# Two-layer hybrid decoder step: the passage from the projections to the attention, reordered

## The chip, the cores and the metric

The kernel runs on one core of one Trainium2 chip. The metric is the device time of one execution in microseconds (us), the median of the runs made; three runs of the kernel before gave 1884.6 us (1883.93 to 1886.74). Engines: PE (TensorE; PEld is its weight load), DVE (VectorE), ACT (ScalarE), POOL (GpSimd) and SP (SyncE), which issues all DMAs.

## The reference

One inference step over 2048 prompt tokens and 64 decode tokens (8 sequences of 8), width 1024, all float32.

```python
# layer 0
a, gl, z = split(rms_norm(x) @ w_in_a, 3)
v = a * sigmoid(gl)                       # causal depthwise convolution, width 31, over positions
c = silu(layer_norm(conv(v))) * silu(z)
x1 = x + c @ w_out_a
# shared keys and values, once
k, v = split(rms_norm(x1, g_kv) @ w_kv, 2)     # 4 heads of 64 each; k = rms_norm(k) per head
# layer 1
q, z = split(rms_norm(x1, g_b) @ w_in_b, 2)    # 16 heads of 64; q = rms_norm(q) per head
s = q @ k.T / 8 - slope * distance             # window of 128 positions, learned sink per head
o = softmax_with_sink(s) @ v
y = x1 + (o * silu(z)) @ w_out_b
```

Outputs are y of prompt and decode tokens, the convolution's last inputs, and the last 128 keys and values of the prompt (`k_p`, `v_p`) and of each decode sequence (`k_s`, `v_s`).

## The kernel before

**Stages.** `phase_a` computes layer 0's input projections and most of the convolution. `phase_b` goes over 17 token tiles (16 of 128 prompt tokens, and tile 16, the 64 decode tokens): for each, LayerNorm, gates, output projection (`out`), residual, RMSNorm, and the projections of k/v and q (`qkv`). Its outputs go to scratch tensors in DRAM: `x1_d`, `kv_d`, `q_d`, and `ht_d`, the normalised and transposed activations in two parts. `phase_c` goes over the 16 prompt tiles: it loads q, k, v and `ht_d` of the tile, transposes q and k on PE, computes the layer-1 gate z, attention, and the layer-1 output projection of the tile before; the decode sequences are fitted in between. Each engine runs its own instruction list; the lists are joined by semaphores, and the order on each engine is the order in which the functions below are called.

**Projections** (`project`, L119). Each float32 operand is cut into a high and a low part, and a 512-column projection is 24 matmuls of three products over 8 slices of the contraction. Weights are cut once: SP loads 256 KB pieces into a staging buffer (`split_weights_dma`, L84), ACT writes the high part (`split_weights_hi`, L99), DVE the low part (`split_weights_lo`, L107). With s stages, a piece's load waits until DVE is through with the piece s before it. A 1024x512 weight matrix is 8 pieces.

**Weight slots.** Five slots of 32 KB per partition. In `phase_b` they hold OUT0, OUT1, KVS, Q0, Q1, in this order; slot 4 is its own tile `b_w`. In `phase_c` slots 0 and 1 hold the gate weights Z0 and Z1, slots 2 and 3 the output weights OUT0 and OUT1, and the memory of slot 4 holds attention's working tiles: the transposed q (`c_qt`) and k (`c_kt`), the scores (`c_s`), the gate (`c_sz`) and others. The staging buffer of the gate weights has 3 stages and lies in `b_cz`; the one of the output weights has 4 and lies over `b_ht`.

**Passage, before.** The last steps of `phase_b` treat tile 15's q and k (`queries`, `keys`, `query_sums`) and tile 16. PE: `out(16)`, `qkv(15)`, `turn_h(16)` (L1248), `qkv(16)`, then `turn_q(0)` (L1868) and `turn_k(0, 0)` (L1874), then the first attention tile: `qk(0)` (L1937), `z(0, 0)`, `qk(1)`, `turn_p(0)` (L1946), `z(0, 1)`, `pv(0)` (L1955, L1961), `qk(2)`, `turn_p(1)`, `pv(1)`, the decode tokens' turns (L1881) and gate projections (`decode_z`), and so on. ACT copies the transposed q and k out of PSUM (L1541, L1545) after its last step of `phase_b`, `queries(16)`, which waits for `qkv(16)`. SP: all 16 gate pieces, with the loads of tile 0 (`first_loads`) before the last 5; the store of `ht_d` of tile 16; then a wait for that store and for the last matmul of `qkv(16)`, 4 output-weight pieces, the stores of tile 16 (among them 16 small ones to `k_s` and `v_s`), 7 loads for the decode tokens, the loads of tile 1, and the further output-weight pieces. ACT and DVE cut the output weights two pieces at a time (`split(0)`, `split(2)`, ... in the bodies of `phase_c`) between the steps of the first attention tile; `split(0)` stands ahead of the first scores on DVE (L1687) and the first exponentials on ACT (L1559, L1561), `split(4)` ahead of the second exponentials.

## Time and profile before

| | |
|---|---|
| median of 3 runs | 1884.6 us |
| the profiled execution's own time | 1884.13 us |
| its span in the trace | 1882.3 us |
| PE busy | 1748.9 us (93%) |
| mean granted TensorE clock | 0.97 of full |
| `phase_b`, tiles | from 0.69 ms to 1.22 ms of the span |
| `phase_c` | from 1.22 ms to the end |

Times in the rows below are microseconds from the span's start. PEclk is the granted TensorE clock, 1.00 for 2.4 GHz and 0.50 for 1.2 GHz; a stretch between holds both.

### The profile page before, as it was taken

The numbers are of one execution on the slowest core, as the hardware profiler recorded it, in microseconds if no ns is written. First come the engines' busy times: TensorE is split into PE (matmuls) and PEld (weight loads), VectorE is DVE, ScalarE is ACT, GpSimd is POOL, SyncE is SP. The second block draws the span as 40 slices with busy tenths as digits, with TensorE's granted clock in tenths as the row PEclk, the third lists the DMA queues.
The fourth block names the chain that finished last, engine by engine and source line by source line (L and its number), as shares of the span: only waits on it lengthen the run. The fifth ranks groups of instructions, "written<-read, shape, count | busy, mean of one in ns | idle before, by whom it ended". The sixth has DMA issues, their size and how long they took to land.

```text
span 1882.3 us, 25336 instructions
## 1 busy us (share of the span) xinstructions
PE 1748.9 (93%) x9105; PEld 1421.9 (76%) x9105; DVE 1199.6 (64%) x2013; ACT 848.6 (45%) x1658; POOL 590.9 (31%) x446
## 2 busy tenths in 40 slices
PE   7999999999997377999999999779999999999998
PEld 6798988888886356787888887557777777777776
DVE  6378889898997445785666643345555556655553
ACT  5555655555563352232323232345444554445442
POOL 2399999999993002221121211100000000000000
PEclk9999999999999588999999999979999999999999
DMA  6221211111212545334444432552221232222311
GB/s 200 81 73 39 73 37 51 57 44 61 64 39 100 167 137 202 137 109 123 137 134 131 148 124 100 175 162 87 82 87 64 76 107 72 93 71 82 101 49 40
DMA packets 157228, 184.47 MB, mean 98 GB/s; under 512 B 55189, under 2 KB 120829, under 8 KB 152972
## 3 DMA queue, kind: packets, MB, share of 16 engines
q1 hardware_dynamic: 157116, 183.00, 30.0%
q8 instruction: 67, 1.10, 0.2%
q14 instruction: 45, 0.37, 0.1%
HBM read 115.31 MB, written 70.34 MB: 99 GB/s over the span
## 4 chain that ended last, share of the span: by engine, by line
PE 54%; DMA 5%; DVE 3%; ACT 2%; SPq 1%; issue 1%; POOL 1%; DVEq 0%; ACTq 0%; POOLq 0%
PE c_acc L119 19%; PE b_pso L119 12%; PE b_psq L119 9%; PE c_pss L1937 3%; PE c_psp L1946 3%; PE c_pso L1961 3%; DMA ht_d<-b_ht 1%; PE b_pst L1248 1%; DVE b_x L1114 1%; PE c_pso L1955 1%; PE b_psc L1242 1%; PE c_pst L1868 1%; DMA b_cz<-in_w_in_b 1%; PE c_pss L119 1%; DMA b_three<-v_left 1%
## 5 line engine op out<-in xcount | busy, mean ns | idle before, releaser
L687 PE MATMUL a_ps<-a_xt,a_wring 128*128 128x512 f32 (+3 forms) x2880 | 556.4, 354 | 13.6 <-ACT a_zo L509 9.3
L687 PEld LDWEIGHTS a_ps<-a_xt,a_wring 128*128 128x128 f32 x2880 | 494.3, 189 | 70.3 <-ACT a_zo L509 11.4
L446 POOL TENSOR_TENSOR a_csum<-a_prod,a_csum 128x704 f32<-128x704 f32 (+1 forms) x242 | 425.5, 1758 | 42.9 <-ACT a_prod L496 7.5
L588 DVE SCALAR_TENSOR_TENSOR a_pst<-a_vbuf,taps,a_pst 128x704 f32<-128x704 f32 (+1 forms) x352 | 327.6, 931 | 11.0
L496 ACT ACTIVATE a_prod<-a_vbuf,taps 128x704 f32<-128x704 f32 (+1 forms) x264 | 225.7, 865 | 182.5 <-POOL a_csum L446 168.5
L119 PE MATMUL b_pso<-w,b_yt 128*128 128x512 f32 (+1 forms) x816 | 193.1, 396 | 0.3 <-DVE b_yt L1108 0.3
L119 PE MATMUL c_acc<-w,c_ht 128*128 128x512 f32 x768 | 185.9, 398 | 0.2 <-issue 0.2
L119 PEld LDWEIGHTS b_pso<-w,b_yt 128*128 128x128 f32 (+1 forms) x816 | 151.7, 188 | 35.3 <-DVE b_yt L1108 0.7
L119 PE MATMUL c_acc<-w,c_ot 128*128 128x512 f32 x720 | 172.0, 394 | 0.0
L119 PEld LDWEIGHTS c_acc<-w,c_ht 128*128 128x128 f32 x768 | 143.3, 190 | 36.5 <-issue 7.3
L119 PEld LDWEIGHTS c_acc<-w,c_ot 128*128 128x128 f32 x720 | 132.9, 188 | 32.5 <-issue 5.8
L1567 ACT ACTIVATE c_pt<-c_psp 128x1024 f32<-128x1024 f32 (+1 forms) x64 | 63.9, 998 | 141.0 <-PE c_psp L1946 141.0
L1561 ACT ACTIVATE c_s<-c_s,c_nm 128x256 f32<-128x256 f32 (+1 forms) x256 | 124.5, 488 | 0.1
L119 PE MATMUL b_pso<-w,b_ht 128*128 128x512 f32 (+1 forms) x408 | 102.6, 409 | 10.3 <-DVE b_x L1114 7.9
L119 PE MATMUL b_psq<-b_w,b_ht 128*128 128x512 f32 (+1 forms) x408 | 99.1, 398 | 5.5 <-DVE b_w L107 5.4
L119 PEld LDWEIGHTS b_pso<-w,b_ht 128*128 128x128 f32 (+1 forms) x408 | 77.6, 194 | 31.6 <-issue 12.5
L1687 DVE SCALAR_TENSOR_TENSOR c_s<-c_dist,c_pss 128x256 f32<-128x256 f32 (+1 forms) x256 | 88.1, 406 | 15.1 <-PE c_pss L1937 14.0
L948 POOL TENSOR_TENSOR b_hms<-b_hss,rms_eps 128x4 f32<-128x4 f32 (+3 forms) x34 | 9.7, 285 | 274.5 <-DVE b_hss L1142 159.6
L119 PE MATMUL b_psq<-w,b_ht 128*128 128x512 f32 (+1 forms) x408 | 95.3, 389 | 0.0
L119 PEld LDWEIGHTS b_psq<-b_w,b_ht 128*128 128x128 f32 (+1 forms) x408 | 76.1, 188 | 25.4 <-DVE b_w L107 8.2
L1006 ACT ACTIVATE b_qo<-b_x 128x1024 f32<-128x1024 f32 (+1 forms) x17 | 18.0, 1061 | 167.6 <-DVE b_x L1114 167.6
L119 PEld LDWEIGHTS b_psq<-w,b_ht 128*128 128x128 f32 (+1 forms) x408 | 75.3, 185 | 17.3
(182 smaller groups left out, 2158.7 us busy)
## 6 DMA issues: line engine op xcount, KB each, us to landing
ht_d<-b_ht SPq DMA_DIRECT2D x16, 1024.0 KB, 4.7
c_ht<-ht_d SPq DMA_DIRECT2D x16, 1024.0 KB, 4.8
a_stage<-in_w_in_a SPq DMA_DIRECT2D x24, 512.0 KB, 4.0
a_x<-in_x_prompt SPq DMA_DIRECT2D x16, 512.0 KB, 3.4
b_cz<-c_d SPq DMA_DIRECT2D x16, 512.0 KB, 4.9
b_cz<-z_d SPq DMA_DIRECT2D x16, 512.0 KB, 6.7
b_x<-in_x_prompt SPq DMA_DIRECT2D x16, 512.0 KB, 3.5
x_d<-b_x SPq DMA_DIRECT2D x16, 512.0 KB, 2.6
```

What stands on the lines that cost most here:

```text
L119: last = pe.matmul(out, xt[:, a, k, 0:n], w[:, b, k], start=(k == 0 and a == 0 and b == 0), stop=(k == KT - 1 and b == 1))
L446: pool.tensor_tensor(out, prod[:, (PTAPS * n + i) % RING, 0:t1 - t0], out, ALU.add).then_inc(prod_added, 1)
L496: act.activation(prod[:, m % RING, 0:t1 - t0], vbuf[:, b % 2, t0 + k:t1 + k], ACT.Identity, scale=wcol(k, b), bias=bcol(b) if i == 0 else ...
L588: dve.scalar_tensor_tensor(part if k == DTAPS - 1 else here, vbuf[:, b % 2, t0 + k:t1 + k], wcol(k, b), part if k == 0 else here, ALU.mult ...
L687: last = pe.matmul(out, wring[:, u % 3, a, k], xt[c][:, e, k, 0:n], start=(k == 0 and a == 0 and e == 0), stop=(k == KT - 1 and a == 1))
L1114: dve.tensor_tensor(x[0:n], ps_o[0:n], x[0:n], ALU.add).then_inc(x1_ready, 1)
L1561: ins = act.activation(s[:, b, j, ks], s[:, b, j, ks], ACT.Exp, bias=nm[:, b, j:j + 1], accum_out=den[:, b, j:j + 1])
L1567: act.activation(pt[:, ks], ps_p[:, ks], ACT.Copy).then_inc(pt_ready, 1)
L1687: ins = dve.scalar_tensor_tensor(s[:, b, place(j), ks], dist[:, gap], -slope[kv * GROUP + j], ps_s[:, place(j), ks], ALU.mult, ALU.add)
L1937: ins = pe.matmul(ps_s[:, place(j), keys_of(t)], qt[e * HD:(e + 1) * HD, h // 2], keys[:, keys_of(t)], start=True, stop=True)
L1946: ins = pe.transpose(ps_p[:, half, j], s[:, b, j, half * P:(half + 1) * P], g.ident[:, :])
L1961: ins = pe.matmul(ps_o[e * HD:(e + 1) * HD, 0:2 * P], v[:, half, kv * HD:(kv + 1) * HD], pt[:, half, 2 * e:2 * e + 2], start=(half == 0), ...
```

## The change

Six things are altered, all around the end of `phase_b` and the first attention tile:

1. **Slots.** KVS goes to slot 4 and Q1 to slot 2. So attention's tiles lie over the k/v weights, which are last read by the first 24 matmuls of `qkv(16)`.
2. **Turns inside.** `turn_q(0)` and `turn_k(0, 0)` are issued on PE inside `qkv(16)`, between its k/v and its q projections; ACT's copies of them follow its `keys_values(16)`.
3. **Order.** Tile 15's q steps come later on ACT and DVE, behind `cut_h(16)`; the body of tile 16 ends before them. ACT and DVE cut the gate weights in the order 5, 3, 2, 6 pieces between these steps.
4. **Gate weights.** A staging buffer of 4 stages, over two stages of `b_three` and half of `b_cz`; pieces are counted on `phase_c`'s semaphores (0 to 15), output weights after them (16 to 31).
5. **SP's queue.** Tile 0's q is loaded once x1 of tile 16 is stored, its k after `turn_h(16)`, the rest of its loads after gate piece 11. `kv_d` of tile 16 is stored before the wait for the last q matmul; SP waits for that store to land and then writes `k_s` and `v_s` with 2 DMAs from `kv_d` to DRAM in place of 16. The output-weight pieces go 6 (of which 2 wait for stages), then the store of q and the decode loads, then 2 more ahead of tile 1's loads, then the rest.
6. `qscale` is computed at the start of `phase_b`; small tiles (sinks and others) get other places.

The core of the diff:

```diff
@@ phase_b
-    OUT0, OUT1, KVS, Q0, Q1 = range(5)
+    OUT0, OUT1, Q1, Q0, KVS = range(5)
-    gate_stage = cz[:, 0:w.stages * HALF].rearrange("p (s n) -> p s n", s=w.stages)
+    gate_stage = nc.alloc_sbuf_tensor_at("b_gate", [P, 4, HALF], F32, offset=g.w_base + 4 * g.slot_bytes + p.at["three"] + 4 * HALF)
@@ phase_b, sync: body(t)
+            if isinstance(t, int) and t == TILES:
+                for done in (ht_out, q_out, kv_out):
+                    sp.wait_ge(done, 16 * (TILES - 1))
...
             if isinstance(t, int) and t == TILES:
-                sp.wait_ge(tc_done, ALL)
-                sp.wait_ge(prod_ready, ALL)
-                w.stage = gate_stage
-                split_weights_dma(sp, io.w_in_b[:, D:D + HALF], w, 3)
-            if not (isinstance(t, int) and t == 0):
-                store_qkv(t - 1)
+                return
+            store_kvq(t - 1)
@@ phase_b, sync: the end
-        split_weights_dma(sp, io.w_in_b[:, D + HALF:2 * D], w, 4, k1=w.stages)
-        sp.wait_ge(ht_out, 16 * TILES)
-        sp.wait_ge(q_out, 16 * TILES)
-        sp.wait_ge(kv_out, 16 * TILES)
+        sp.wait_ge(tc_done, ALL)
+        sp.wait_ge(prod_ready, ALL)
+        gates(0, 4)
         sp.wait_ge(x1_out, 16 * ALL)
+        sp.wait_ge(h_ready, ALL)
+        load_queries()
+        store_kvq(TILES - 1)
+        sp.dma_start(io.k_p, kvo[:, 0:KV]).then_inc(copy_out, 16)
+        sp.dma_start(io.v_p, kvo[:, KV:2 * KV]).then_inc(copy_out, 16)
+        gates(4, 8)
         sp.wait_ge(th_done, ALL)
-        first_loads()
-        split_weights_dma(sp, io.w_in_b[:, D + HALF:2 * D], w, 4, k0=w.stages)
+        load_keys()
         store_ht(ALL - 1)
-        p.store_last = lambda: store_qkv(ALL - 1)
+        gates(8, 12)
+        load_rest()
+        store_q(TILES - 1)
+        gates(12, 16)
+        store_kvq(ALL - 1)
+        sp.wait_ge(kv_out, 16 * ALL)
+        for to, cols in ((io.k_s, slice(0, KV)), (io.v_s, slice(KV, 2 * KV))):
+            sp.dma_start(to[:, P - DS:P, :], g.kv_d[SEQ:TOK, cols].rearrange("(b i) n -> b i n", b=DB)).then_inc(copy_out, 16)
+        p.store_last = lambda: store_q(ALL - 1)
@@ phase_b, scalar: the end
         steady(act, body)
+        act.wait_ge(out_mm, ALL)
+        gates(0, 5)
         cut_h(ALL - 1)
-        split_weights_hi(act, 0, gains[Q0], w, 3, k0=5)
-        split_weights_hi(act, 1, gains[Q0], w, 4, k1=w.stages)
+        queries(TILES - 1)
+        gates(5, 10)
         keys_values(ALL - 1)
-        split_weights_hi(act, 1, gains[Q0], w, 4, k0=w.stages)
+        turned()
+        gates(10, 16)
         queries(ALL - 1)
@@ phase_b, vector: the end
         steady(dve, body)
+        gates(0, 5)
         cut_h(ALL - 1)
-        queries(ALL - 2)
-        split_weights_lo(dve, 0, gains[Q0], w, 3, k0=5)
-        split_weights_lo(dve, 1, gains[Q0], w, 4, k1=w.stages)
+        query_sums(TILES - 1)
+        gates(5, 8)
+        queries(TILES - 1)
+        gates(8, 10)
         keys(ALL - 1)
-        split_weights_lo(dve, 1, gains[Q0], w, 4, k0=w.stages)
+        gates(10, 16)
         query_sums(ALL - 1)
@@ phase_b, tensor
             project(pe, ps_o[0:n, 0:HALF], ht, w.wslot[KVS], n, (w.w_lo, 0) if gate else None).then_inc(kv_mm, 1)
+            if between is not None:
+                between()
             after(pe, q_ready, t)
@@ phase_c, sync
-        split_weights_dma(sp, io.w_out_b[:, 0:HALF], w, 0, k1=w.stages)
+        w.stage = stg
+        split_weights_dma(sp, io.w_out_b[:, 0:HALF], w, 2, k1=6)
         prev.store_last()
         sp.wait_ge(prev.q_out, 16 * ALL)
-        sp.wait_ge(prev.kv_out, 16 * ALL)
-        sp.wait_ge(prev.w.w_lo, 5 * KT)
+        sp.wait_ge(w.w_lo, 2 * KT)
...
+            if first:
+                split_weights_dma(sp, io.w_out_b[:, 0:HALF], w, 2, k0=6)
             if not last:
                 load_q(t + 1)
                 load_k(t + 1, 1 - r)
             if first:
-                split_weights_dma(sp, io.w_out_b[:, 0:HALF], w, 0, k0=w.stages)
                 load_v(1, 1)
+                split_weights_dma(sp, io.w_out_b[:, HALF:D], w, 3, k1=4)
                 load_ht(1)
-                split_weights_dma(sp, io.w_out_b[:, HALF:D], w, 1)
+                split_weights_dma(sp, io.w_out_b[:, HALF:D], w, 3, k0=4)
@@ phase_c, scalar and tensor
+        def turned():
+            act.wait_ge(prev.qscale_made, 1)
+            queries(0)
+            keys(0, 0)
+        def first_turns():
+            turn_q(0)
+            turn_k(0, 0)
-        prev.tensor(pe)
-        turn_q(0)
-        turn_k(0, 0)
+        prev.tensor(pe, first_turns)
```

`gates(first, stop)` loads, or cuts the high or low parts of, the gate-weight pieces from `first` up to `stop`; `store_kvq(t)` stores `kv_d` and, for tiles before 15, `q_d`; `load_rest` loads the distance tables, the sinks, `ht_d` and v of tile 0.

## Rows read from the trace of the kernel before

**Rows 1.** The page: PE's busy time, the chain that ended last by engine.
```profile
PE 1748.9 (93%) x9105; PEld 1421.9 (76%) x9105; DVE 1199.6 (64%) x2013; ACT 848.6 (45%) x1658; POOL 590.9 (31%) x446
...
PE 54%; DMA 5%; DVE 3%; ACT 2%; SPq 1%; issue 1%; POOL 1%; DVEq 0%; ACTq 0%; POOLq 0%
```
**Rows 2.** Windows of 1300 to 1882 us: busy us per engine, PEclk, DMA share, GB/s.
```profile
1300.00:1882.00 582.00, 571.70 (x3273) 427.56 (x3271) 318.04 (x812) 267.69 (x757) 0.00 (x0) 1.00 0.23 77
```
**Rows 3.** Timeline, PE, end of phase_b: start, duration, operation, count, idle before.
```profile
1177.33 5.70 PE L119 MATMUL b_pso<-w,b_ht 128*128 128x512 f32 x24 [1.40 <-DVE b_x L1114]
1182.87 5.60 PE L119 MATMUL b_psq<-w,b_ht 128*128 128x512 f32 x24
...
1196.88 7.30 PE L119 MATMUL b_pso<-w,b_ht 128*64 128x512 f32 x24 [2.32 <-DVE b_ht L1119]
1204.02 5.68 PE L119 MATMUL b_psq<-w,b_ht 128*64 128x512 f32 x24
```
**Rows 4.** Timeline, DVE, between the transposes of tile 16 and its projections.
```profile
1195.00 1.22 DVE L1142 TENSOR_REDUCE b_hss<-b_qo 128x16 f32<-128x1024 f32 x1 [2.43 <-ACT b_qo L1038]
1196.14 0.68 DVE L1119 TENSOR_TENSOR b_ht<-b_pst,b_ht 128x512 fp32r<-128x512 f32 x1
1199.54 1.23 DVE L1148 TENSOR_TENSOR b_qo<-b_psq,b_hrs 128x1024 f32<-128x1024 f32 x1 [2.72 <-POOL b_hrs L950]
```
**Rows 5.** Timeline, PE, the passage and the first attention tile up to `z(0, 1)`.
```profile
1215.05 1.04 PE L1868 MATMUL c_pst<-ident,c_q 128*128 128x128 f32 x8
1215.93 0.60 PE L1874 MATMUL c_acc<-ident,c_kd 128*128 128x128 f32 x4
1225.23 1.23 PE L1937 MATMUL c_pss<-c_kt,c_qt 64*128 64x128 f32 x8 [8.70 <-ACT c_kt L1545]
1226.38 8.03 PE L119 MATMUL c_acc<-w,c_ht 128*128 128x512 f32 x24
1234.35 0.72 PE L1937 MATMUL c_pss<-c_kt,c_qt 64*128 64x128 f32 x8
1234.99 0.66 PE L1946 MATMUL c_psp<-ident,c_s 128*128 128x128 f32 x4
1235.87 5.72 PE L119 MATMUL c_acc<-w,c_ht 128*128 128x512 f32 x24 [0.22 <-issue]
```
**Rows 6.** Windows, the first gate projection, `z(0, 0)`; columns as in rows 2.
```profile
1226.40:1234.40 8.00, 8.00 (x28) 6.10 (x26) 3.62 (x10) 3.61 (x11) 0.26 (x1) 0.70 0.35 98
```
**Rows 7.** Timeline, SP's DMA issues: time of issue, time issuing, what.
```profile
1217.07 0.62 SPq L829 DMA_DIRECT2D ht_d<-b_ht  x1
1222.32 1.75 SPq L84 DMA_DIRECT2D c_stg<-in_w_out_b  x4
...
1231.18 0.47 SPq L856 DMA_DIRECT2D q_d<-b_qo  x1
...
1241.25 1.93 SPq L84 DMA_DIRECT2D c_stg<-in_w_out_b  x4
```
**Rows 8.** Timeline, ACT, in the first attention tile.
```profile
1226.35 0.63 ACT L99 ACTIVATE w<-c_stg 128x512 fp32r<-128x512 f32 x1 [0.75 <-DMA c_stg<-in_w_out_b]
1229.69 1.28 ACT L1559 ACT_TABLE_LOAD   x1 [2.71 <-DVE c_es L1698]
...
1234.45 0.60 ACT L1553 ACTIVATE c_sz<-c_acc 128x512 f32<-128x512 f32 x1 [1.72 <-PE c_acc L119]
...
1246.03 1.38 ACT L99 ACTIVATE w<-c_stg 128x512 fp32r<-128x512 f32 x2 [9.46 <-DMA c_stg<-in_w_out_b]
```
**Rows 9.** Timeline, PE, after the second stop of the first attention tile.
```profile
1249.10 1.12 PE L1946 MATMUL c_psp<-ident,c_s 128*128 128x128 f32 x4 [6.05 <-ACT c_s L1561]
...
1255.09 7.33 PE L119 MATMUL c_acc<-w,c_otd 128*64 128x512 f32 x24
...
1263.82 5.74 PE L119 MATMUL c_acc<-w,c_otd 128*64 128x512 f32 x24 [0.15 <-DVE c_early L1732]
```
**Rows 10.** DMA issues, 1140 to 1300 us: tile 16's store to `kv_d`, KB, us to landing.
```profile
kv_d<-b_three SPq DMA_DIRECT2D x1, 128.0 KB, 5.0
```

More of the change, by code:

```diff
@@ L1268, in out, with qkv @@
             ins.then_inc(out_mm, 1)
-        def qkv(t, gate=False):
+        def qkv(t, gate=False, between=None):
             n = rows_of(t)
@@ L1339, in phase_c @@
     nsink = sb("c_nsink", [P, HEADS])
+    small[0] = prev.at["three"] + 4 * HALF
     sinkd = sb("c_sinkd", [P, 2])
```

100 lines of the change are left out of this document (52 added, 48 removed).

## The prediction

> **What bounds the kernel now.** The page comes first: PE is busy 93% of the span and carries 54% of the chain that ended last, all others together a quarter of that [rows 1]. So time is gained only where PE stands still or runs slowly. The windows come next: from 1300 us on PE is busy 571.7 of 582 us at the full clock [rows 2]. Nothing there is touched by the change, so what is gained ahead of it is carried to the end unchanged. Last comes PE's timeline through the passage. The reader is to see four things. Tile 16's k/v projection waits 2.32 us and then starts to start takes 7.14 us (1196.88 to 1204.02), where tile 15's takes 5.54 (1177.33 to 1182.87) [rows 3]. After the turns of q and k PE stands for 8.70 us, on ACT's copy of k [rows 5]. The gate projection behind it takes 7.97 us, at a mean clock of 0.70: part of it ran at 1.2 GHz [rows 6]. And PE stops again for 6.05 us before the second `turn_p`, with a projection of 7.33 us following [rows 9]. These are about 17 us of standing and 6 us of slow clock.
>
> The sum is made against the profiled execution (1884.13 us). It lies 0.5 below the median of 1884.6, and I add that back at the end.
>
> **Part 1: tile 16's cut goes ahead of tile 15's q.** In the kernel before, DVE reduces tile 15's squares at 1195.00 (1.22 us) and only then makes the low part of tile 16 at 1196.14; PE follows 0.74 us later [rows 4]. PE had finished the transposes at 1194.56 (1196.88 less 2.32). After the change the chain is ACT's high part (a 512-column copy, 0.60 [rows 8]) plus the handover, DVE's cut at 1195.2, PE at 1195.95. Removed: 0.93 us. The clock: PE resumed at full speed after 1.40 us of standing, at half speed after 2.32 [rows 3]. The new stop is 1.39 us, nearest to the first, so I take 5.54 us instead of 7.14: 1.60 more (bounds 0 and 1.60). PE starts the k/v part at 1195.95 and ends it at 1201.49.
>
> What is moved here must still be in time. Five gate pieces stand ahead of `cut_h(16)` on ACT. The fifth has to wait for a stage; it is loaded once DVE has cut the first (about 1187) and SP has stored tile 15's k and v (until 1187.6), so it lands near 1191.5 and is cut by 1192.3, 2 us ahead of the transposes. Tile 15's query chain (squares, reduction, POOL, product) took 4.54 us from reduction to product [rows 4]. Now the reduction is at 1196.1, so the product is at 1200.65 and ends at 1201.9; PE wants `q_ready` at 1202.9. Slack 1.0 us, and the three gate pieces that DVE takes meanwhile (1197.3 to 1199.3) fit in. On SP, `ht_d` of tile 15 now waits for a landing, some 2.5 us, which nobody misses before 1194.
>
> **Part 2: turns inside the last projection, copies over the k/v slot.** The turns cost PE the same 1.48 us (1215.05 to 1216.53 [rows 5]), now in front of the q part: 1.38 start to start. q was asked for at about 1180.5 and k at 1194.6, and PE turns them at 1201.5 and 1202.4; a load of such a kind lands in about 5 us, so neither is waited for. The q part takes 11.03 us as before (1204.02 [rows 3] to 1215.05 [rows 5]). Its end: 1195.95 + 5.54 + 1.38 + 11.03 = 1213.9. ACT's copies are done at about 1205, under this projection. So the 8.70 us go wholly: the first scores start at 1213.9 instead of 1225.23, and at the full clock take 0.64 (1234.35 to 1234.99) instead of 1.15 [rows 5]. The gate projection starts at 1214.5 and ends at 1220.1, in 5.54 us instead of 7.97. Up to here 14.3 us are gained (1234.35 less 1220.1). The cover: the eight pieces of Z0 are cut by about 1199, those of Z1 by 1214.
>
> **Part 3: what is late next.** Scores need their distance step and exponentials, and ahead of them on DVE and ACT stands `split(0)`: two output-weight pieces. Their staging lies over tile 16's activations, so SP can't ask for them before the last q matmul, 1213.9. In the kernel before SP asked at 1222.32, after the landing of the `ht_d` store issued at 1217.07 [rows 7]; now that store goes at 1196. SP has a new wait, on the landing of `kv_d` of tile 16. Issued at about 1207.9 it lands 5.0 us later by its own row [rows 10], 1212.9; the two DRAM copies behind it aren't in the rows, and I take one issue of 0.44 each (1.75/4 [rows 7]), bounds 0.3 and 1.0. SP is ready at 1213.8. So the piece chain moves by 8.3 us and no more, while PE has moved by 14.3: the exponentials, which ended 3.04 us after the table load began (1229.69 [rows 8], so 1232.73), end at 1224.45. PE, done with `qk(1)` at 1220.95, stands until 1224.55. This is a **new wait of 3.6 us**. Then `turn_p(0)`, ACT's tanh, DVE's product and `z(0, 1)`: 1.42 us from tanh to projection (1234.45 [rows 8], 1235.87 [rows 5]), hence 1225.8. The clock falls, since 3.6 us is longer than the stop of 2.32. After 8.70 us it cost about 3.0 us (0.51 + 2.43); after 2.32 it cost 1.6. I take 2.0 on `z(0, 1)` (bounds 0 and 3.0), ending at 1233.4.
>
> The Trainium skill (DMA: Bandwidth & Descriptors, Anatomy of one DMA) gives a DMA 2.0 us of fixed cost plus its bytes at 436 GB/s, fitted on another issue path. By my estimate from it a 256 KB piece lands in 2.6 us, where the row of ACT's wait has 3.7 (second piece, issued at about 1222.7, cut at 1226.35 [rows 7, 8]). By the page the new wait would be 2.6 us instead of 3.6, and the total 1 us lower; the row is used.
>
> **Part 4: the second stop.** It was `split(4)`: ACT's pieces 4 and 5 came at 1246.03, asked for at 1241.25 behind everything SP did from 1224 on [rows 7, 8]. Six pieces are now asked for ahead of that work; the last two wait only for DVE's first two cuts (about 1219.5). So the 6.05 us and the slow clock behind them go. What is late next is `split(6)` on ACT: pieces 6 and 7 stand behind the q store, its landing and seven decode loads. With the three loads of tile 1's q and k these took from 1231.18 to 1241.25 [rows 7]; now the q store goes at 1222.5, so the two are asked for at 1230.9 to 1231.8 and land at about 1235 to 1236. ACT cuts them, then copies the second transposed scores: PE waits about 1.0 us (bounds 0 and 3). From 1233.4: `pv(0)` 0.9, `qk(2)` 0.65, `turn_p(1)` and the gate's transposes 0.95, the wait 1.0, `pv(1)` 0.65, the decode turns 0.85: the first `decode_z` at 1238.45 instead of 1255.09. It takes 5.55 instead of 7.33, and the next starts at 1245.7 after its usual 1.5 us handover, instead of 1263.82 [rows 9]. **18.1 us.** Later output pieces come with 3 us or more in hand.
>
> **The sum.** 0.93 + 1.60 (part 1), + 8.70 + 0.51 + 2.43 (part 2), + 0.1 of rounding at the turns: 14.3. New wait and slow clock in part 3: -6.2 (1241.4, where `z(0, 1)` ended, less 1233.4 leaves 8.0). Part 4: 6.05 of standing, 2.0 of waiting for the gate product, 1.8 on the projection, 1.3 on small matmuls, less 1.0: +10.1. In all 18.1, hence 1884.1 - 18.1 = 1866.0, and with 0.5 for the median 1866.5 us. Against an error of 0.2% (3.8 us), about what a measurement of this kernel can tell from no change, this is far off zero.
>
> **Rivals.** (a) *SP comes late to the output pieces.* The wait for `kv_d`, or the DRAM copies behind it, last 3 to 5 us longer, or pieces 6 and 7 land later behind the many small decode packets. Each microsecond beyond 1213.9 lengthens the new stop by one. For it: SP's slack is 0.1 us by my reckoning. Against: the store has little beside it. Time 1870.5. The skill speaks for it (same page, same section): the write receipt makes the completion of a DMA that writes HBM surprisingly long. The row's 5.0 us already holds that, beside other traffic.
> (b) *The clock stays at 2.4 GHz* at the new stop, because the pieces land sooner and the stop falls towards 2 us. For it: a stop of 1.40 did no harm. Time 1863.5.
> (c) *The slow clock holds on* (the other side). After the new stop come further short stops (the gate handover, 1.0, 0.5 us), and PE remains at 1.2 GHz up to the end of tile 1's gate projections. In rows 6, 4.8 us at half clock and 3.2 at full did 24 matmuls and some; that is near 11 us for a projection at half clock, 5.4 too many. Five projections add 27 us, less the 2.0 counted, and the small matmuls about 5: 30 us, 1896. It turns slower than before from about three and a half projections on. Against: at 1226.4 the clock came back within one projection.
> (d) *Nothing arrives*: tile 1 would have to wait for its own loads, which stand behind more pieces than before. They need an 18 us delay; q and k are asked for at 1232 and used at 1255. Time 1884.
>
> **Chances.** Forecast 0.70 (1863.5 to 1869), (a) 0.13, (b) 0.11, (c) 0.03, (d) 0.03. The range 1862.5 to 1871.0 takes in (a) and (b) and the bounds above: upwards 1.6 for the clock in part 1, 1.0 in part 3 and 2 in part 4, not all at once. Faster 0.95, same 0.02, slower 0.03.
>
> **What would show it.** Right: tile 16's k/v projection after a stop of about 1.4 us in 5.5 to 5.7 us; no stop after the turns, which stand between k/v and q; `z(0, 0)` in 5.6 us; a stop of about 3.6 us before the first `turn_p`, released by ACT's exponentials; no stop over 2 us after it; from 1245 on the old pattern, 18 us sooner. Wrong: a wait on `q_ready` inside `qkv(16)` (part 1), q or k landing late (part 2), ACT waiting for a piece more than 2 us at `split(6)` (part 4), a clock at half speed through `decode_z` (c).

## The result: 18.2 us faster

| | before | changed |
|---|---|---|
| median | 1885.67 us (4 runs, 1883.93 to 1887.31) | 1867.46 us (4 runs, 1865.19 to 1870.01) |
| the profiled execution's own time | 1884.13 us | 1867.84 us |
| its span | 1882.3 us | 1866.0 us |

The ratio is 0.9904 with a 95% interval of 0.9887 to 0.9921. Forecast were 1866.5 us for the median and 18.1 us of gain. The two profiled executions differ by 16.3 us. The one of before was itself 1.5 below its median, the other 0.4 above.

The page of the changed kernel, PE's busy time and the chain that ended last (rows 1 of before). PE is busy 5.4 us less with the same matmuls, since fewer of them run at the slow clock. The chain's shares barely moved, though nearly 1% of the time has gone.

```profile
PE 1743.5 (93%) x9105; PEld 1421.5 (76%) x9105; DVE 1198.8 (64%) x2013; ACT 847.9 (45%) x1658; POOL 591.2 (32%) x446
...
PE 54%; DMA 4%; DVE 3%; ACT 3%; issue 1%; SPq 1%; POOL 0%; DVEq 0%; ACTq 0%; POOLq 0%
```

A window of the changed kernel over the attention (start:end, length, busy us and instructions per engine, PEclk, DMA share, GB/s). It answers rows 2: PE is busy 570.4 of 581 us at the full clock, as before. What was gained ahead of it was carried to the end.

```profile
1285.00:1866.00 581.00, 570.42 (x3266) 426.56 (x3262) 317.52 (x812) 267.65 (x757) 0.00 (x0) 1.00 0.23 77
```

PE's timeline of the changed kernel through the passage (start, duration, operation, count, idle before and its releaser). It answers rows 3, 5 and 9.

```profile
1164.78 11.29 PE L119 MATMUL b_pso<-w,b_yt 128*64 128x512 f32 x48
...
1196.13 5.73 PE L119 MATMUL b_pso<-b_w,b_ht 128*64 128x512 f32 x24 [1.41 <-DVE b_ht L1132]
1201.70 1.04 PE L1903 MATMUL c_pst<-ident,c_q 128*128 128x128 f32 x8
1202.57 0.60 PE L1909 MATMUL c_acc<-ident,c_kd 128*128 128x128 f32 x4
1202.93 11.29 PE L119 MATMUL b_psq<-w,b_ht 128*64 128x512 f32 x48
1214.14 0.72 PE L1972 MATMUL c_pss<-c_kt,c_qt 64*128 64x128 f32 x8
1214.79 5.75 PE L119 MATMUL c_acc<-w,c_ht 128*128 128x512 f32 x24
1221.87 0.72 PE L1972 MATMUL c_pss<-c_kt,c_qt 64*128 64x128 f32 x8 [1.33 <-DVE c_s L1717]
1226.10 1.08 PE L1981 MATMUL c_psp<-ident,c_s 128*128 128x128 f32 x4 [3.51 <-ACT c_s L1583]
1227.25 7.92 PE L119 MATMUL c_acc<-w,c_ht 128*128 128x512 f32 x24
...
1238.25 0.65 PE L1996 MATMUL c_pso<-c_pt,c_v 128*64 128x256 f32 x4 [0.82 <-ACT c_pt L1589]
...
1239.59 5.75 PE L119 MATMUL c_acc<-w,c_otd 128*64 128x512 f32 x24
...
1247.28 5.74 PE L119 MATMUL c_acc<-w,c_otd 128*64 128x512 f32 x24 [0.70 <-DVE c_early L1762]
...
1259.94 5.74 PE L119 MATMUL c_acc<-w,c_ht 128*128 128x512 f32 x24
```

The reader is to see this. The stop ahead of tile 16's k/v projection (1196.13) is 1.41 us instead of 2.32, and the projection runs at full speed. The turns (1201.70, 1202.57) stand between k/v and q without a stop. The first scores follow the q part at once (1214.14), where 8.70 us were lost. Then come two stops that were not there, 1.33 and 3.51 us, with a slow `z(0, 1)` behind them (7.92 us). The 6.05 us of rows 9 are gone, and 0.82 us is what is left ahead of the second `pv`.

For comparisons between kernels one measure is used below, **the passage**: from the start of tile 16's output projection (b_yt, 128*64) to the start of tile 1's first gate projection. In the changed kernel it is 1259.94 - 1164.78 = 95.16 us. In the kernel before it ran between these two rows of PE's timeline, 111.85 us. So it is 16.7 us shorter by the rows. Where two kernels are compared inside the passage, times are counted from its start, which differs by up to 6.6 us between the traces. It leaves out what happens ahead of it in an execution.

```profile
1164.64 11.29 PE L119 MATMUL b_pso<-w,b_yt 128*64 128x512 f32 x48
...
1276.49 5.73 PE L119 MATMUL c_acc<-w,c_ht 128*128 128x512 f32 x24
```

SP's DMA issues in the changed kernel (time of issue, time issuing, what), answering rows 7:

```profile
1204.19 4.95 SPq L84 DMA_DIRECT2D b_gate<-in_w_in_b  x4
1209.24 0.48 SPq L849 DMA_DIRECT2D kv_d<-b_three  x1
1213.42 0.78 SPq L953 DMA_DIRECT2D out_k_s<-kv_d  x1
1214.24 0.73 SPq L953 DMA_DIRECT2D out_v_s<-kv_d  x1
1215.09 6.20 SPq L84 DMA_DIRECT2D c_stg<-in_w_out_b  x6
```

and ACT in the first attention tile, answering rows 8:

```profile
1217.65 0.63 ACT L99 ACTIVATE w<-c_stg 128x512 fp32r<-128x512 f32 x1 [2.38 <-DMA c_stg<-in_w_out_b]
1219.58 0.63 ACT L99 ACTIVATE w<-c_stg 128x512 fp32r<-128x512 f32 x1 [1.29 <-DMA c_stg<-in_w_out_b]
1222.91 1.28 ACT L1581 ACT_TABLE_LOAD   x1 [2.71 <-DVE c_es L1728]
...
1227.85 1.14 ACT L99 ACTIVATE w<-c_stg 128x512 fp32r<-128x512 f32 x2
```

SP comes to the output-weight pieces at 1215.09. The second of them is cut on ACT at 1219.58, after a wait for its landing. Only then can DVE do the scores' distance step, and ACT loads its table at 1222.91. `turn_p` starts at 1226.10. That is the new wait. The fifth and sixth piece (1227.85) are cut without any.

### The profile page after: what moved, and what is told of

It reads as the page before. It is cut to its first block, busy times and chain, and to the rows that moved or that the text cites. A ratio compares the mean times of both kernels' runs of the same rounds, so it can differ in the third digit from the quotient of the medians.

```text
span 1866.0 us, 25323 instructions
## 1 busy us (share of the span) xinstructions
PE 1743.5 (93%) x9105; PEld 1421.5 (76%) x9105; DVE 1198.8 (64%) x2013; ACT 847.9 (45%) x1658; POOL 591.2 (32%) x446
## 4 chain that ended last, share of the span: by engine, by line
PE 54%; DMA 4%; DVE 3%; ACT 3%; issue 1%; SPq 1%; POOL 0%; DVEq 0%; ACTq 0%; POOLq 0%
PE c_acc L119 19%; PE b_pso L119 12%; PE b_psq L119 9%; PE c_pss L1972 3%; PE c_psp L1981 3%; PE c_pso L1996 3%; PE b_pst L1262 1%; DMA ht_d<-b_ht 1%; DVE b_x L1127 1%; PE c_pso L1990 1%; PE b_psc L1256 1%; PE c_pst L1903 1%; PE c_pss L119 1%; DMA b_three<-v_left 1%; DMA c_stg<-in_w_out_b 1%
## 5 line engine op out<-in xcount | busy, mean ns | idle before, releaser
L119 PE MATMUL b_psq<-w,b_ht 128*128 128x512 f32 (+1 forms) x816 | 189.9, 391 | 4.7 <-DVE w L107 4.7
L119 PEld LDWEIGHTS b_psq<-w,b_ht 128*128 128x128 f32 (+1 forms) x816 | 150.6, 185 | 40.6 <-DVE w L107 6.5
L119 PE MATMUL b_pso<-b_w,b_ht 128*128 128x512 f32 (+1 forms) x408 | 102.3, 408 | 9.3 <-DVE b_x L1127 7.9
L119 PEld LDWEIGHTS b_pso<-b_w,b_ht 128*128 128x128 f32 (+1 forms) x408 | 78.0, 195 | 29.8 <-issue 10.6
L960 POOL TENSOR_TENSOR b_hms<-b_hss,rms_eps 128x4 f32<-128x4 f32 (+3 forms) x34 | 10.1, 297 | 265.3 <-DVE b_hss L1155 158.3
L1750 DVE TENSOR_TENSOR c_sz<-c_pso,c_sz 128x256 f32<-128x256 f32 x64 | 27.1, 424 | 93.7 <-ACT c_sz L1594 93.7
L1178 DVE SCALAR_TENSOR_TENSOR b_conv<-b_conv,taps 128x64 f32<-128x64 f32 x240 | 68.2, 284 | 19.6 <-DVE b_conv L1178 1.1
```

Of the source, the lines that this page charges most:

```text
L119: last = pe.matmul(out, xt[:, a, k, 0:n], w[:, b, k], start=(k == 0 and a == 0 and b == 0), stop=(k == KT - 1 and b == 1))
L1178: dve.scalar_tensor_tensor(out, win, scalar(g.taps, k * KT), out, ALU.mult, ALU.add).then_inc(left_step, 1)
```

## The experiments

**One part undone: tile 15's squares ahead of tile 16's cut** (`cut_behind_q`).

```diff
@@ phase_b, scalar
-        cut_h(ALL - 1)
         queries(TILES - 1)
+        cut_h(ALL - 1)
@@ phase_b, vector
-        cut_h(ALL - 1)
         query_sums(TILES - 1)
+        cut_h(ALL - 1)
```

> The changed kernel with one part undone: on ACT and DVE tile 15's squares and their sums stand ahead of tile 16's cut again. Theory A (the first exponentials hang on output-weight pieces that SP asks for once the last q matmul is done and its own queue is free, at 1215.1 us, 0.95 us after the last q matmul at 1214.14): tile 16's k/v projection starts 0.9 us later after a stop of 2.3 us and takes 7.1 instead of 5.6 us, since the clock falls; the q part ends 2.5 us later, of which SP's 0.95 us swallow a part, so tile 1's first gate projection comes 1.6 us later than in the changed kernel (1259.94). Theory B (PE's own work sets the end throughout): 2.5 us later. If the clock doesn't fall: A 0.0, B 0.9.

PE's timeline of this kernel, tile 16's k/v projection:

```profile
1198.10 7.33 PE L119 MATMUL b_pso<-b_w,b_ht 128*64 128x512 f32 x24 [2.32 <-DVE b_ht L1132]
```

Its stop and its 7.33 us are those of rows 3. The passage is 96.62 us, 1.46 more than in the changed kernel, where theory A gave 1.6 and B 2.5. Median 1868.38 us, ratio to before 0.9917 (0.9900 to 0.9933). Part 1 removes 2.5 us of PE's time and is worth 1.5 by this trace. The rest is swallowed on SP: here it asks for the output pieces 0.14 us after the last q matmul (1217.85 and 1217.71), in the changed kernel 0.95 us after it, so its request moves by only 1.7 us. In the timing the difference of 0.0013 between the ratios (about 2.5 us) lies within the intervals.

**The turns behind the whole last projection again** (`turns_after`).

```diff
@@ phase_b, scalar
-        turned()
         gates(10, 16)
+        turned()
@@ phase_c, tensor
-        prev.tensor(pe, first_turns)
+        prev.tensor(pe, None)
+        first_turns()
```

> The changed kernel with the turns of tile 0's q and k put behind the whole last projection again, and ACT's copies behind its last gate piece; the slots stay as changed. PE's first scores start about 1.9 us later than 1214.14, at 1216.0, after a stop of 1.8 us. Theory A (pieces set the first exponentials, 4.8 us of standing behind them on PE): the stops before the first turn_p shrink by 1.9 us, and tile 1's first gate projection starts within 0.3 us of the changed kernel's 1259.94. Theory B (PE's own work sets the end): 1.9 us later.

PE's timeline: the q part, the first scores, the first `turn_p`, `z(0, 1)`, the second `pv` and the first `decode_z`.

```profile
1202.93 11.26 PE L119 MATMUL b_psq<-w,b_ht 128*64 128x512 f32 x48 [1.05 <-DVE b_qo L1161]
...
1216.90 0.71 PE L1972 MATMUL c_pss<-c_kt,c_qt 64*128 64x128 f32 x8 [1.41 <-ACT c_kt L1567]
...
1226.03 0.63 PE L1981 MATMUL c_psp<-ident,c_s 128*128 128x128 f32 x4 [2.11 <-ACT c_s L1583]
1227.19 5.73 PE L119 MATMUL c_acc<-w,c_ht 128*128 128x512 f32 x24 [0.53 <-issue]
...
1237.80 0.65 PE L1996 MATMUL c_pso<-c_pt,c_v 128*64 128x256 f32 x4 [2.62 <-ACT c_pt L1589]
...
1239.37 7.04 PE L119 MATMUL c_acc<-w,c_otd 128*64 128x512 f32 x24
```

The first scores come at 1216.90, 2.8 us later than in the changed kernel, where 1.9 were expected. Yet `turn_p` comes at 1226.03, in the same place to 0.1 us (both traces have the output projection at 1164.8). The stop ahead of it has shrunk from 3.51 to 2.11, the one before `qk(1)` is gone. `z(0, 1)` then runs at full speed, and the clock falls for the first `decode_z` instead. The passage is 95.68 us, 0.52 more. That is over the 0.3 that theory A allowed and far under the 1.9 of B, and no more than two traces of the changed kernel differ by. The trace shows why PE's lateness is lost again: ACT stood 1.13 and 0.72 us for pieces 6 and 7 ahead of the copy that the second `pv` waits for, and the first `decode_z` starts 74.58 us after the output projection, in the changed kernel 74.81. So theory A's mechanism holds: the part of the change that its name puts foremost is worth next to nothing in this trace, since something else sets the first exponentials and the second `pv`. The timing can't confirm so small a cost: median 1868.66, ratio 0.9918 (0.9902 to 0.9935), 0.0014 or 2.6 us above the changed kernel's with intervals that overlap. The row at 1202.93 shows one thing more. PE waits 1.05 us for `q_ready` ahead of the q part; in the changed kernel the turns fill just that wait.

**SP's order of output pieces as before the change** (`four_pieces_first`).

```diff
@@ phase_c, sync
-        split_weights_dma(sp, io.w_out_b[:, 0:HALF], w, 2, k1=6)
+        split_weights_dma(sp, io.w_out_b[:, 0:HALF], w, 2, k1=4)
...
-            if first:
-                split_weights_dma(sp, io.w_out_b[:, 0:HALF], w, 2, k0=6)
             if not last:
                 load_q(t + 1)
                 load_k(t + 1, 1 - r)
             if first:
+                split_weights_dma(sp, io.w_out_b[:, 0:HALF], w, 2, k0=4)
                 load_v(1, 1)
-                split_weights_dma(sp, io.w_out_b[:, HALF:D], w, 3, k1=4)
                 load_ht(1)
-                split_weights_dma(sp, io.w_out_b[:, HALF:D], w, 3, k0=4)
+                split_weights_dma(sp, io.w_out_b[:, HALF:D], w, 3)
```

> The changed kernel with SP's order of output pieces as before the change: four pieces, the q store, the decode loads, q and k of tile 1, and only then the fifth piece. Theory A (ACT's fifth and sixth piece stand ahead of the second exponentials, and their request is what made the second stop): pieces asked for at about 1234, cut at about 1239, second exponentials done at 1241.6, PE stands some 5 us before the second turn_p and runs slowly after it; tile 1's first gate projection 6 to 8 us later than 1259.94, whole time 1873.5 to 1875.5. Theory B (that stop was a follow-up of the first one and is gone with it): under 2 us later.

PE's timeline, the second `turn_p` and the first `decode_z`; then SP's request for the fifth piece:

```profile
1241.22 1.11 PE L1979 MATMUL c_psp<-ident,c_s 128*128 128x128 f32 x4 [6.49 <-ACT c_s L1581]
...
1247.22 7.26 PE L119 MATMUL c_acc<-w,c_otd 128*64 128x512 f32 x24
```

```profile
1232.15 1.93 SPq L84 DMA_DIRECT2D c_stg<-in_w_out_b  x4
```

The second stop is back with 6.49 us, released by the exponentials, and the slow clock after it, 7.26 us for a projection. Passage 105.48 us, 10.3 more than the changed kernel, where 6 to 8 were expected; median 1876.35, ratio 0.9961 (0.9947 to 0.9976). ACT cuts the fifth piece after 12.17 us of standing, ended by that piece's landing. The mechanism is that of part 4, and the size is what part 4 had put on it (10.1), not the smaller figure of this expectation: the stop was 6.49 us instead of some 5, and another stop of 1.98 us for the gate product follows, which it doesn't name.

**The same order put into the kernel before, alone** (`before_six_pieces`): the diff above, reversed, on the kernel before.

> The kernel before with SP's order of output pieces alone changed (6 pieces ahead of the stores and decode loads, 2 behind them, then q and k of tile 1). Theory A (ACT's fifth piece made the second stop; pieces 6 and 7, asked for at about 1242 behind 16 small stores and the decode loads, are late next): no stop before the second turn_p, one of about 4 us before the second pv; 106 to 108 us on the measure of split0_late, where the kernel before has 111.85; total 1879 to 1881. Theory B (this part is worth by itself what its absence cost in four_pieces_first, 10.3 us): 101.5 us, total 1874.5.

PE's timeline, the second `pv`:

```profile
1248.76 1.12 PE L1963 MATMUL c_pso<-c_pt,c_v 128*64 128x256 f32 x4 [4.77 <-ACT c_pt L1569]
```

Passage 108.21 us, 3.6 less than before; median 1879.37, ratio 0.9975 (0.9965 to 0.9985). That is 0.2 us outside theory A's 106 to 108 and far from B's 101.5. So this part costs 10.3 us where it is missing from the change, but gives only 3.6 where it is added alone: in the kernel before, pieces 6 and 7 stand behind the 16 small stores as well, ACT waits 2.90 and 1.08 us for them, and a stop of 4.77 us takes the place of the one of 6.05. The parts don't add up, and here the timing agrees: by the ratios the same two steps are 0.0057 (10.7 us) and 0.0025 (4.7 us), each clear of its interval.

**The three stages** (`three_stages`): a gate piece is asked for only when the piece three before it is cut.

```diff
@@ phase_c, sync, gates
             for k in range(first, stop):
+                after(sp, w.w_lo, k - 2)
                 split_weights_dma(sp, ...)
```

> The changed kernel with gate piece k asked for only when piece k-3 is cut, as with three stages. Theory A (the gate weights have slack everywhere but ahead of tile 16's cut): SP holds q's load and the k/v store back by about 1 us, the fifth piece lands 1 to 1.5 us later, still ahead of the transposes' end; 95.2 to 95.7 us on the measure of split0_late. Theory B (four stages carry the result): the fifth piece comes later than the transposes, tile 16's cut waits, and the clock falls: 97 us or more.

SP's issues: the last four gate pieces, the k/v store, the output pieces. Then PE: tile 16's k/v projection, `qk(1)`, `turn_p(0)` and `z(0, 1)`.

```profile
1209.77 10.86 SPq L84 DMA_DIRECT2D b_gate<-in_w_in_b  x4
1220.72 0.48 SPq L849 DMA_DIRECT2D kv_d<-b_three  x1
...
1225.55 6.20 SPq L84 DMA_DIRECT2D c_stg<-in_w_out_b  x6
```

```profile
1197.47 7.26 PE L119 MATMUL b_pso<-b_w,b_ht 128*64 128x512 f32 x24 [2.68 <-DVE b_ht L1132]
...
1232.32 1.23 PE L1973 MATMUL c_pss<-c_kt,c_qt 64*128 64x128 f32 x8 [8.93 <-DVE c_s L1718]
1236.55 1.08 PE L1982 MATMUL c_psp<-ident,c_s 128*128 128x128 f32 x4 [3.00 <-ACT c_s L1584]
1237.71 7.62 PE L119 MATMUL c_acc<-w,c_ht 128*128 128x512 f32 x24
```

Theory A was wrong, and B, which had said only 97 us or more, was right for the smaller part: passage 105.68 us, 10.5 more; median 1877.58, ratio 0.9967 (0.9956 to 0.9978). What B said did happen, a cut that comes late (2.68 us of standing, then 7.26 us at a slow clock), but it makes the first scores only 2.8 us later. The larger part is in SP's queue. The last four gate pieces take SP from 1209.77 to 1220.63, where the changed kernel needs 1204.19 to 1209.14, since each request waits for the cut of the piece three before it, not four, and behind them stand the k/v store and the output pieces. These are asked for at 1225.55 instead of 1215.09, 10.5 us later, and the first scores' step with them: PE stands 8.93 us ahead of `qk(1)`. The gate weights themselves were never late: `z(0, 0)` ran without a stop.

**The output pieces ahead of the k/v store's wait and the copies** (`pieces_before_copies`).

```diff
@@ phase_b, sync, the end
         store_kvq(ALL - 1)
-        sp.wait_ge(kv_out, 16 * ALL)
-        for to, cols in ((io.k_s, ...), (io.v_s, ...)):
-            sp.dma_start(to[:, P - DS:P, :], g.kv_d[SEQ:TOK, cols]...)
-        p.store_last = lambda: store_q(ALL - 1)
+        def store_last():
+            sp.wait_ge(kv_out, 16 * ALL)
+            for to, cols in ((io.k_s, ...), (io.v_s, ...)):
+                sp.dma_start(to[:, P - DS:P, :], g.kv_d[SEQ:TOK, cols]...)
+            store_q(ALL - 1)
+        p.store_last = store_last
```

> The changed kernel with the wait for tile 16's k/v store and the two DRAM copies moved behind the six output pieces. Theory A (SP's lateness of 0.95 us at these pieces is passed on in full to the first exponentials): pieces asked for at 1214.35 instead of 1215.09, first turn_p at 1225.35 instead of 1226.10, tile 1's first gate projection 0.7 us earlier. Theory B (the landing, not the request, decides, because other traffic is in the way): no difference, or later, since the copies now run beside the fifth piece.

ACT's cut of the second piece. This trace runs 1.10 us later up to here (the output projection starts at 1165.88).

```profile
1219.04 0.63 ACT L99 ACTIVATE w<-c_stg 128x512 fp32r<-128x512 f32 x1 [0.52 <-DMA c_stg<-in_w_out_b]
```

Passage 93.60 us, 1.56 less: theory A in direction, with twice its 0.7. SP asks at 1215.38, in the changed kernel's time 1214.28, 0.81 earlier. The second piece is cut at 1217.94 in that time instead of 1219.58, 1.64 earlier. So half of what the cut gains is the request, the other half a shorter time from request to landing: 3.66 us instead of 4.49. That the copies made the difference is borne out by the next run, which has no copies and 3.68 us, and by the other five traces with the two copies directly ahead, which have 4.01 to 4.49. Median 1865.67, ratio 0.9901 (0.9883 to 0.9919); against the changed kernel's 0.9904 that isn't a difference that the timing alone could show.

**The copies replaced by 16 small stores** (`sixteen_stores`), with the wait for the k/v store ahead of the q store.

```diff
@@ phase_b, sync, the end
-        sp.wait_ge(kv_out, 16 * ALL)
-        for to, cols in ((io.k_s, ...), (io.v_s, ...)):
-            sp.dma_start(to[:, P - DS:P, :], g.kv_d[SEQ:TOK, cols]...)
+        for b in range(DB):
+            sp.dma_start(io.k_s[b, P - DS:P, :], kvo[rows, 0:KV])
+            sp.dma_start(io.v_s[b, P - DS:P, :], kvo[rows, KV:2 * KV])
```

> The changed kernel with k_s and v_s written by 16 small stores in the place of the two DRAM copies, and the wait for the k/v store moved ahead of the q store. Theory A (the two copies brought nothing in their place: the store at 1209.24 plus 16 issues of 0.34 us ends at 1215.2, the wait and the copies end at 1215.05): 95.2 us within 0.5 on the measure of split0_late. Theory B (the copies' own traffic or the small stores' traffic delays the two pieces that are waited for): 0.8 us or more to either side.

The output pieces in SP's issues (the output projection starts at 1168.09 here):

```profile
1219.61 5.40 SPq L84 DMA_DIRECT2D c_stg<-in_w_out_b  x6
```

They are asked for 51.5 us after the output projection's start, in the changed kernel 50.3. The passage is 95.69 us, 0.53 more; median 1870.28, ratio 0.9927 (0.9907 to 0.9948). In the place where they stand, the wait and two copies save 1.2 us of SP's time over the 16 stores. But the second piece is cut 3.68 us after the request instead of 4.49, so the cut itself comes only 0.4 us later (55.20 and 54.80 us after the start). Theory A's "brought nothing" is right for the end, though not for SP's queue; a difference of 0.53 us in the passage is no more than two traces of one kernel show.

**The changed kernel a second time** (`changed_again`), on the same chip as `sixteen_stores` and `reordered_turns_after`.

> The changed kernel itself, beside the two below. On the measure of split0_late it took 95.16 us in its profile; the first stops hang on landings, so 94.5 to 96.5 us is expected here. The two profiled executions of before and after differ by 16.3 us, the medians by 18.2: if that is scatter of single executions alone, this one again gives a ratio between 0.9887 and 0.9921.

PE's timeline, tile 16's k/v projection:

```profile
1195.76 7.30 PE L119 MATMUL b_pso<-b_w,b_ht 128*64 128x512 f32 x24 [1.41 <-DVE b_ht L1132]
```

Median 1867.17, ratio 0.9909 (0.9890 to 0.9927), passage 95.71 us. The stop is 1.41 us as in the first trace, but this time the clock fell after it, and the projection took 7.30 us instead of 5.73. All the same the passage is only 0.55 us longer, within the 94.5 to 96.5 expected. SP asked for the output pieces 0.84 us later (1215.56; the second copy took 1.42 us of issuing here), the stops ahead of the first `turn_p` shrank from 4.84 to 3.92 us, and `z(0, 1)` lost 0.6 us less to its slow clock (7.32 us instead of 7.92).

**The first two pieces cut behind the first exponentials** (`split0_late`).

```diff
@@ phase_c, scalar
-            split(0)
             exps(t * KVH, 0, ks)
             gate_tanh(t, 0)
+            split(0)
             split(2)
@@ phase_c, vector
-            split(0)
             scores(G, t, 0, 0, r)
...
             gate(t, 0)
+            split(0)
             scores(G + 1, t, 1, 1, r)
```

> The changed kernel with the first two output-weight pieces cut behind the first exponentials and the first gate product on ACT and DVE, SP's order unchanged. Measured from the start of tile 16's output projection to the start of tile 1's first gate projection, the kernel before takes 111.85 us, the changed one 95.16. Theory A (removing the new stop only uncovers the next transfer: pieces 6 and 7 are asked for behind the q store and the decode loads at about 1233, and ACT has them ahead of the second pv): the stop before the first turn_p falls from 4.84 to about 1 us, z(0,1) starts 4 us earlier and at full clock, and PE then stands 5 to 7 us before the second pv; 95 to 97 us, so no gain. Theory B (the new stop was the last one that counts): 88 to 90 us.

PE's first `turn_p`, `z(0, 1)` and second `pv`, then ACT's seventh piece:

```profile
1226.84 0.63 PE L1981 MATMUL c_psp<-ident,c_s 128*128 128x128 f32 x4 [0.77 <-ACT c_s L1583]
1227.99 5.72 PE L119 MATMUL c_acc<-w,c_ht 128*128 128x512 f32 x24 [0.53 <-issue]
...
1244.44 1.12 PE L1996 MATMUL c_pso<-c_pt,c_v 128*64 128x256 f32 x4 [5.74 <-ACT c_pt L1589]
```

```profile
1241.93 0.63 ACT L99 ACTIVATE w<-c_stg 128x512 fp32r<-128x512 f32 x1 [6.04 <-DMA c_stg<-in_w_out_b]
```

The new wait is gone: 0.77 us ahead of `turn_p`, and `z(0, 1)` at the full clock. But PE then stands 5.74 us ahead of the second `pv`, while ACT waits for the seventh piece, which is behind the decode loads in SP's queue. Passage 98.55 us, 3.4 more than the changed kernel; median 1871.77, ratio 0.9936 (0.9920 to 0.9953). Theory A in its mechanism, and 1.6 us beyond its upper end: there is a second stop of 2.44 us ahead of that `pv`, and the clock falls for `decode_z`.

**All pieces behind the attention's steps, decode loads ahead of the fifth** (`reordered`): as `split0_late` and `pieces_before_copies`, and

```diff
@@ phase_c, sync
-        split_weights_dma(sp, io.w_out_b[:, 0:HALF], w, 2, k1=6)
+        split_weights_dma(sp, io.w_out_b[:, 0:HALF], w, 2, k1=4)
...
-                split_weights_dma(sp, io.w_out_b[:, 0:HALF], w, 2, k0=6)
+                split_weights_dma(sp, io.w_out_b[:, 0:HALF], w, 2, k0=4)
@@ phase_c, scalar: order in the first body
+            exps0, tanh0, split(0), split(2), turn_out0, exps1, tanh1, copy_gate0, turn_out1,
+            exps2, copy_gate1, split(4), decode_first, split(6), decode_tanh(0), turn_out2,
+            split(8), exps3, split(10), decode_tanh(1), ...
@@ phase_c, vector: likewise, split(4) and split(6) behind norm2, split(8) behind scores3, split(10) behind norm3
```

> As split0_late, and in addition: SP asks for 4 pieces, then makes the DRAM copies, the q store and the decode loads, and asks for pieces 4 to 7 behind these; ACT and DVE cut pieces 4 to 11 behind the second and third exponentials instead of ahead of them. Theory A (every output piece can wait, attention's steps and the decode loads can't): no stop over 1.5 us in the first attention tile, the clock stays at 2.4 GHz, 88 to 90 us on the measure of split0_late, total 1860 to 1862.5. Theory B (the decode loads bound it, since the q store waits for POOL's power): PE stands 2 to 4 us before the decode turns, 91 to 93 us, total 1864.

PE's timeline of the first attention tile (the output projection starts at 1165.04), and a window over it, with PEclk third from the end:

```profile
1222.21 0.63 PE L1985 MATMUL c_psp<-ident,c_s 128*128 128x128 f32 x4 [0.77 <-ACT c_s L1586]
1223.37 5.71 PE L119 MATMUL c_acc<-w,c_ht 128*128 128x512 f32 x24 [0.53 <-issue]
...
1231.80 0.65 PE L2000 MATMUL c_pso<-c_pt,c_v 128*64 128x256 f32 x4 [0.47 <-ACT c_pt L1592]
...
1233.14 5.75 PE L119 MATMUL c_acc<-w,c_otd 128*64 128x512 f32 x24
```

```profile
1222.00:1260.00 38.00, 34.76 (x199) 23.70 (x199) 27.06 (x66) 26.28 (x73) 0.00 (x0) 1.00 0.64 193
```

No stop over 0.8 us in the first attention tile, the clock at 1.00 throughout, passage 88.20 us, 7.0 less than the changed kernel. Median 1861.06 us, ratio 0.9884 (0.9868 to 0.9901). Theory A in every number: this version beats both kernels, the changed one by 7.0 us in the rows and by 6.4 us in the medians (of different sets of runs). By the ratios it is 0.0020 (3.8 us), and the intervals overlap a little; still, the slowest of its four executions (1863.06) is faster than the fastest of the changed kernel's eight (1864.13). The version joins several moves; of these only `split0_late` (3.4 us worse) and `pieces_before_copies` (1.6 us better) were run by themselves.

**And there the turns behind the projection** (`reordered_turns_after`): the diff of `turns_after` on `reordered`.

> The kernel reordered (88.20 us on the measure of split0_late) with the turns of q and k behind the whole last projection. In turns_after they cost 0.5 us, since PE stood afterwards anyway. Theory A (the stop that covered them is gone, so they now cost what ACT's copies take): 1.3 to 1.9 us more, 89.5 to 90.1, with a stop of 1.4 us before the first scores. Theory B (they are free wherever they stand, since something else still sets the first exponentials): under 0.6 us more.

PE: the q part and the first scores.

```profile
1204.74 11.26 PE L119 MATMUL b_psq<-w,b_ht 128*64 128x512 f32 x48 [1.05 <-DVE b_qo L1164]
...
1218.71 0.72 PE L1976 MATMUL c_pss<-c_kt,c_qt 64*128 64x128 f32 x8 [1.41 <-ACT c_kt L1570]
```

Passage 92.42 us, 4.2 more, where theory A gave 1.3 to 1.9 and B under 0.6. The rows name 1.05 us ahead of the q part (`q_ready`, which the turns used to fill), 1.41 ahead of the first scores (ACT's copies), and 1.8 us that arise after the second `decode_z`: a stop of 1.21 us where `reordered` has 0.39, and then a slow clock for tile 1's first scores. Ahead of that stop ACT stood 0.65 and 0.21 us for late output pieces, which no row ties to the turns. Up to both `decode_z` it is 2.4 us (the first scores come 2.7 us later, and the stop ahead of `turn_p` shrinks by 0.4), more than theory A's 1.9, because the expectation had left out the wait for `q_ready`. So the same edit that left the first `decode_z` where it was in the changed kernel (0.2 us earlier) puts it 2.4 us later here; the further 1.8 are from one trace and not shown to be its doing. Median 1864.42, ratio 0.9892 (0.9874 to 0.9909), 0.0008 or 1.5 us above `reordered`: the timing can't tell the two apart, and the profiled execution (1867.87) was the slowest of the four.

| kernel | passage, us | median, us | ratio to before |
|---|---|---|---|
| before | 111.85 | 1885.67 | 1 |
| before_six_pieces | 108.21 | 1879.37 | 0.9975 |
| three_stages | 105.68 | 1877.58 | 0.9967 |
| four_pieces_first | 105.48 | 1876.35 | 0.9961 |
| split0_late | 98.55 | 1871.77 | 0.9936 |
| cut_behind_q | 96.62 | 1868.38 | 0.9917 |
| changed_again | 95.71 | 1867.17 | 0.9909 |
| sixteen_stores | 95.69 | 1870.28 | 0.9927 |
| turns_after | 95.68 | 1868.66 | 0.9918 |
| changed | 95.16 | 1867.46 | 0.9904 |
| pieces_before_copies | 93.60 | 1865.67 | 0.9901 |
| reordered_turns_after | 92.42 | 1864.42 | 0.9892 |
| reordered | 88.20 | 1861.06 | 0.9884 |

Passages are from one trace each; the medians are of four sets of runs, of which each has its own runs of the kernel before (medians 1885.67, 1884.91, 1883.69 and 1882.36), so the ratios compare better than the medians. Two traces of the changed kernel differ by 0.55, so differences under about 0.6 us say little. The intervals of the ratios reach 2 to 4 us to either side: they set `before_six_pieces`, `three_stages` and `four_pieces_first` apart from the changed kernel, and none of the others from it.

## Why the prediction held, and where it didn't

The median was forecast at 1866.5 and is 1867.46. By the rows the gain is 16.7 us where the sum had 18.1; the medians' difference of 18.2 agrees with the sum more closely than the working deserves, and that is luck. The sum's last step also has a slip: 1238.45 with 5.55 and 1.5 is 1245.5, not 1245.7, which would make it 18.3.

**Part 1 held.** The stop is 1.41 us (1.39), the projection started at 1196.13 (1195.95), and it took 5.57 us start to start (5.54). That the clock wouldn't fall was a choice between two rows, and a good one: of the nine traces that have this stop of 1.41 us it fell in one, `changed_again`. What the forecast missed is how little it matters: with or without those 1.6 us the passage differs by 0.55. Part 1 was put at 2.5 us; undone alone it is worth 1.5. The slack of 1.0 us that tile 15's query chain was given shrank to nothing: the reduction started 0.2 us later than reckoned, and from it to the product took 5.34 us instead of 4.54. The product ran at 1201.64, a microsecond later than reckoned, and ended at 1202.87, when PE started the q part at 1202.93.

**Part 2 held on PE's side.** The q part ended at 1214.1 (1213.9), no stop for q, k or the copies, `z(0, 0)` in full speed to 1220.5 (1220.1). The 14.3 us were there. But `turns_after` shows that the moved turns were not what the end hung on: with the turns behind the projection the first `decode_z` comes no later. The sum books 8.7 us to part 2 and takes some back in part 3, which is right for the whole and wrong for the parts.

**Part 3 had the right mechanism and too small a size.** The stop ahead of the first `turn_p`, released by the exponentials behind two output pieces, is there: 1.33 + 3.51 = 4.84 us, forecast 3.6. The terms: SP came to the pieces at 1215.09 instead of 1213.9, since the k/v store went out 1.3 us later (1209.24, behind the last gate pieces) and the two copies took 1.5 us of issuing (0.78 and 0.73), not 0.9; and the second piece was cut 4.5 us after the first request instead of 4.0. The store itself landed faster than its row said (at most 4.2 us, from 1209.24 to the next issue at 1213.42, not 5.0). The slow clock cost 2.2 us on `z(0, 1)` (7.77 us start to start against 5.54), forecast 2.0. These misses make 1.6 us, up to `z(0, 1)`'s end at 1235.0 instead of 1233.4.

**Part 4 held,** in both directions. No second stop; the wait ahead of the second `pv` was 0.82 us, forecast 1.0. Its cause was only in part the one given. ACT didn't wait for pieces 6 and 7 to land, it cut them at 1236.31 for 1.40 us ahead of the copy; and `reordered`, where nothing is cut there, still waits 0.47. The first `decode_z` came 15.5 us sooner (16.6). The handover to the second took 0.5 us longer than usual, as ACT stood 2.70 us for pieces 8 and 9 (PE stood 0.70 us there, in `reordered`, where ACT waits for no piece, 0.16); "3 us or more in hand" for the later pieces was wrong.

**Rival (a)**, SP late, came true in part: 1.2 of its 3 to 5 us. The reasons were the late store and the copies' issue time; the wait for the landing was shorter than the row (at most 4.2 us, not 5.0). The Trainium skill (DMA: Bandwidth & Descriptors, Anatomy of one DMA) says that a DMA that writes HBM can complete surprisingly late; in this trace that made nothing late, since the landing was priced by its row and came sooner. The other use of that section can be judged too. Its fixed cost and bandwidth gave, by the prediction's estimate, 2.6 us for a 256 KB piece. The first piece was cut 2.6 us after SP began to ask, so for the first the trace agrees. The second, which is the one waited for, was cut 4.5 us after SP began to ask, with the two copies ahead of it in the same queue and further pieces behind. The row (3.7 us, from the piece's own request) was the better price. **Rival (b)** fell with the longer stop: 4.84 us in all, and the clock fell. **Rival (c)** had nothing: after the new stop the clock came back within one projection. **Rival (d)** neither.

**What the prediction didn't price is the staging buffer.** It called the gate pieces covered and gave the four stages no value of their own; SP was reckoned to be through with them before it stored tile 16's k and v, at 1207.9. `three_stages` shows 10.5 us. The pieces have slack as data, but their requests wait in the queue in which the output pieces, the k/v store and the decode loads stand.

## What to carry to other kernels

When a stop is removed, ask which queue the next wait's data must pass and what blocks that queue. Here SP's order and its staging waits were worth 10 us each, the transposes moved under a projection half a microsecond by the traces. The worth of a part depends on what else is in place: the same edit of SP's order gave 3.6 or 10.3 us; the turns gave nothing or 2.4 us up to the first `decode_z`, the latter by one trace each and within the noise of the timing. Work that can wait, such as cutting weights for a later stage, belongs behind the step that something is waiting for on the same engine, and its loads behind those of that step: that was the last 7 us.
